# Hybrid decoder trunk, one core: group norm by tokens inside the chunk loop, decode step and w_out interleaved, w_out's weights gone over twice

## The chip, the core and the metric

The kernel runs on one core of a Trainium2 chip. The metric is device time in microseconds for one execution of the whole program: two decoder layers and a final norm.

The core has five engines with a queue each, in order: TensorE (PE, matmuls; PEld is its weight load), VectorE (DVE), ScalarE (ACT), GpSimd (POOL) and SyncE (SP, here the issuer of DMAs). They meet only through semaphores. Everything is float32; where a matmul carries weights, each operand is split into a high part (fp32r) and a low part, and three matmuls make one product: high x high, high weight x low activation, low weight x high activation.

## What is computed

Each layer, for 1024 prompt tokens and 8 sample tokens (a decode step) that share the weights:

```
h = rmsnorm(x); proj = h @ w_in
ya = rwkv7_mix(proj[:, :A_PROJ])          # recurrent state per head, 8 heads of 64
yb = sliding_window_attention(proj[:, A_PROJ:])
x = x + concat(ya, yb) @ w_out
h2 = rmsnorm(x); x = x + (silu(h2 @ w_gate) * (h2 @ w_up)) @ w_down
```

The end of `rwkv7_mix` is what moves. `y` is what the state scan reads out per token and head:

```
mean = mean(y over the 64 of a head); var = mean((y - mean)^2)
yn = (y - mean) * rsqrt(var + LNX_EPS) * lnx_g + lnx_b
bonus = sum(r * k * r_k over the head) * v
out = (yn + bonus) * g
```

The sample tokens have a state each (8 x 8 heads x 64 x 64), which takes one step of the same recurrence.

## The kernel before

Activations lie with channels on the 128 partitions and the T = 1032 tokens (1024 prompt, 8 sample) along the free axis. T is cut in three columns of CW = 344 tokens; `cs(c)` is a column. A weight unit is 128 x 1024. SP loads it (`fill_dma`), ScalarE casts its high part (`fill_high`), POOL subtracts the low part (`fill_low`), in a ring of three slots, so unit k + 3 takes the slot of unit k. A `tile` is one unit against one column: 8 k-steps of three matmuls (lines 1455 to 1457), 24 in all.

A layer runs through these stages: w_in (21 units), rope and attention, the preparation of the scan (LoRAs, decays, an inversion of triangular blocks by elimination on VectorE), then the chunk loop (line 1770): 16 chunks of 64 tokens. In chunk n TensorE applies the state to the keys (s1), makes the grams of chunk n + 1, solves (s2), transposes keys and values for the next chunk (`keys`, `values`), forms the state's update (s3) and reads y out (lines 1806 and 1808, channels on the partitions). VectorE masks the grams (line 1215), adds and scales the state (lines 1249 and 1251: S_add, S_new). Until chunk 5 VectorE also runs the elimination for chunks 8 to 15.

After the loop three things follow one another. The decode step: SP loads the states (line 424), VectorE and TensorE go through them in two halves (`i` in 0, 1), with sums over a head's channels as matmuls against `bdones` (lines 1826, 1828, 1831). Then the group norm for all columns, in twelve pieces of 128 channels x 344 tokens: TensorE centres (line 1841), sums squares (1849) and spreads root and bonus back over the channels (1835); ScalarE squares and takes roots; VectorE multiplies and gates (1313 to 1317, 1298); ScalarE casts the high part (814), POOL subtracts the low part (518). Then w_out: 8 units, three columns each (line 1882). It waits for the last low part `fin_low11`; ScalarE's first w_out cast waits for it too (line 819).

Behind w_out VectorE adds each tile to the residual `x`, which SP has loaded back from memory (`x_back`, line 440), ScalarE squares it, VectorE sums the squares (`sum2`), and after the last unit the second norm follows column by column: `inverse` (a reciprocal), `normed`, a cast on ScalarE (`high2`), `low2`. FFN's first tile follows it k-step by k-step (line 1462).

FFN: 11 iterations of 6 units (gate and up for two halves j, then two units of w_down). Per half VectorE makes `mid` for three columns, then `mid_low` for three (lines 1403 to 1406). The down projection waits for `ff{i}_low1{c}` and puts its 24 results in two PSUM banks in turn (four in the last iteration), which VectorE's additions free (line 1415).

## Time and profile before

| | us |
|---|---|
| median of three runs | 3411.71 (3409.21 to 3415.93) |
| the profiled execution | 3412.88 |
| its span, first to last instruction | 3410.9 |
| TensorE busy | 3031.5 (89%) |
| VectorE busy | 1395.1 (41%) |
| ScalarE busy | 849.3 (25%) |
| POOL busy | 568.7 (17%) |
| mean granted TensorE clock | 0.917 |

Times within an execution count from the span's start. A timeline row has its start, its length, engine, line and operation, what it writes and reads, a count where rows are merged, and in brackets the engine's idle time before it and what ended that. TensorE's records are pipelined: the distance of two starts is the cost of a matmul, not a record's length. A float32 matmul leaves two records, a transposition or an fp32r matmul one.

### The profile page before, as it was taken

The page shows a single profiled execution, that of the slowest core. Times are in us where ns is not written, and L with a number is a line of the kernel's source. Part 1 is how long each engine was busy: PE and PEld are TensorE (multiplying, and loading weights), DVE is VectorE, ACT ScalarE, POOL GpSimd, SP SyncE. Part 2 cuts the span into 40 slices and gives each one's busy share as a digit, 9 for nine tenths or more (in the row PEclk, how much of TensorE's full clock was granted, in tenths as well). Part 3 has the DMA queues.
Part 4 walks back from the last instruction along what each step waited for, and adds up shares of the span by engine and source line. Part 5 has one row for each costly group of instructions (what it writes and reads, how often), then busy time and mean ns, then how long its engine had stood idle before and what let it go on. Part 6 is the DMA issues. An engine that isn't in the chain of part 4 may idle for free.

```text
span 3410.9 us, 49606 instructions
## 1 busy us (share of the span) xinstructions
PE 3031.5 (89%) x20894; PEld 2748.5 (81%) x20894; DVE 1395.1 (41%) x2435; ACT 849.3 (25%) x1799; POOL 568.7 (17%) x277
## 2 busy tenths in 40 slices
PE   7996766978999999999999977579789999999997
PEld 6994734853999999999999956358359999999997
DVE  5325549643342232222353275684434223222324
ACT  3102642422231111111321044424223211111112
POOL 2220000002122112121122100100021221221123
PEclk9998967985999999999999988679769999999998
DMA  3101010012111111111121100000121111111111
GB/s 118 46 25 50 0 37 7 2 46 93 44 45 50 44 44 46 48 45 49 65 70 47 42 21 7 31 7 2 70 81 38 50 50 38 50 50 44 44 47 53
DMA packets 49443, 149.13 MB, mean 44 GB/s; under 512 B 8912, under 2 KB 19152, under 8 KB 48208
## 3 DMA queue, kind: packets, MB, share of 16 engines
q1 hardware_dynamic: 49232, 146.07, 13.0%
q8 instruction: 163, 2.67, 0.3%
q14 instruction: 48, 0.39, 0.0%
HBM read 128.52 MB, written 17.54 MB: 43 GB/s over the span
## 4 chain that ended last, share of the span: by engine, by line
PE 81%; DVE 12%; ACT 3%; issue 2%; DMA 1%; SPq 0%; POOL 0%; ACTq 0%; DVEq 0%
PE bank L1455 21%; PE bank L1457 20%; PE bank L1456 20%; PE bank L1835 2%; PE bank L1530 2%; PE bank L1562 1%; PE bank L1680 1%; PE bank L1808 1%; PE bank L1806 1%; PE bank L1523 1%; PE bank L1788 1%; PE bank L1841 1%; PE bank L1711 1%; PE bank L1798 1%; PE bank L1622 1%
## 5 line engine op out<-in xcount | busy, mean ns | idle before, releaser
L1455 PE MATMUL bank<-act_high,w_high 128*128 128x344 f32 x3504 | 1129.9, 322 | 36.0 <-POOL w_low L472 31.6
L1457 PE MATMUL bank<-act_high,w_low 128*128 128x344 f32 x3504 | 1122.1, 320 | 0.0
L1456 PE MATMUL bank<-act_low,w_high 128*128 128x344 f32 x3504 | 1121.6, 320 | 0.0
L472 POOL TENSOR_TENSOR w_low<-w_raw,w_high 128x1024 fp32r<-128x1024 f32 x190 | 483.5, 2552 | 1678.1 <-ACT w_high L547 1678.1
L1455 PEld LDWEIGHTS bank<-act_high,w_high 128*128 128x128 f32 x3504 | 662.3, 189 | 44.7 <-issue 19.2
L1456 PEld LDWEIGHTS bank<-act_low,w_high 128*128 128x128 f32 x3504 | 661.0, 189 | 1.3 <-issue 0.9
L1457 PEld LDWEIGHTS bank<-act_high,w_low 128*128 128x128 f32 x3504 | 661.7, 189 | 0.0
L1357 DVE TENSOR_TENSOR f_mid<-f_silu,bank 128x344 f32<-128x344 f32 x132 | 67.6, 512 | 849.5 <-PE bank L1457 849.5
L1455 PE MATMUL bank<-f_mid_high,w_high 128*128 128x344 f32 x1056 | 340.8, 323 | 27.2 <-DVE f_mid_low L1362 24.7
L1415 DVE TENSOR_TENSOR resid<-bank,resid 128x344 f32<-128x344 f32 x528 | 272.4, 516 | 223.7 <-PE bank L1457 223.7
L1457 PE MATMUL bank<-f_mid_high,w_low 128*128 128x344 f32 x1056 | 339.5, 321 | 0.0
L1456 PE MATMUL bank<-f_mid_low,w_high 128*128 128x344 f32 x1056 | 336.6, 319 | 0.0
L547 ACT CAST w_high<-w_raw 128x1024 fp32r<-128x1024 f32 x190 | 195.8, 1043 | 511.7 <-PE bank L1457 506.8
L1455 PEld LDWEIGHTS bank<-f_mid_high,w_high 128*128 128x128 f32 x1056 | 198.2, 188 | 33.6 <-issue 32.8
L1456 PEld LDWEIGHTS bank<-f_mid_low,w_high 128*128 128x128 f32 x1056 | 198.3, 188 | 0.2
L1457 PEld LDWEIGHTS bank<-f_mid_high,w_low 128*128 128x128 f32 x1056 | 198.2, 188 | 0.0
L976 DVE TENSOR_TENSOR proj<-bank,s_rstd 128x344 f32<-128x344 f32 x126 | 64.2, 515 | 290.7 <-PE bank L1457 290.7
L856 ACT CAST f_mid_high<-f_mid 128x344 fp32r<-128x344 f32 x132 | 63.3, 480 | 407.6 <-DVE f_mid L1357 407.6
L849 ACT ACTIVATE f_silu<-bank 128x344 f32<-128x344 f32 x132 | 60.0, 457 | 339.1 <-PE bank L1457 339.0
L1530 PE MATMUL bank<-a_k_twice,a_q_spread 128*128 (+1 forms) x256 | 73.1, 438 | 15.8 <-ACT a_q_spread L622 15.1
L1328 DVE TENSOR_TENSOR resid<-bank,resid 128x344 f32<-128x344 f32 x48 | 24.6, 513 | 144.8 <-PE bank L1457 144.8
L1215 DVE TENSOR_TENSOR c_gram<-bank,consts 128x512 f32<-128x512 f32 x64 | 41.2, 685 | 97.1 <-PE bank L1680 97.0
(273 smaller groups left out, 3104.5 us busy)
## 6 DMA issues: line engine op xcount, KB each, us to landing
w_raw<-wts SPq DMA_DIRECT2D x190, 512.0 KB, 3.5
resid<-x SPq DMA_DIRECT2D x3, 1376.0 KB, 11.1
att_keep<-act_low SPq DMA_DIRECT2D x2, 2064.0 KB, 10.6
att_low_back<-att_keep SPq DMA_DIRECT2D x2, 2064.0 KB, 9.4
resid<-x SPq DMA_DIRECT2D x8, 516.0 KB, 6.4
x_keep<-resid SPq DMA_DIRECT2D x3, 1376.0 KB, 5.7
resid<-x_keep SPq DMA_DIRECT2D x8, 516.0 KB, 6.7
o_y<-resid SPq DMA_DIRECT2D x3, 1376.0 KB, 5.7
```

Of the source, the lines that this page charges most:

```text
L472: eng.tensor_tensor(wl[s][:, :], raw[s][:, :], wh[s][:, :].bitcast(F32), ALU.subtract).then_inc(w_low, 1)
L547: eng.copy(wh[s][:, :], raw[s][:, :]).then_inc(w_high, 1)
L849: a(sil[:, c, :], bank[c][:, 0:CW], ACT.Silu).then_inc(scalar_steps, e.step(f"ff{i}_sil{j}{c}"))
L856: eng.copy(mh[:, j, cs(c)], midf[:, c, :]).then_inc(scalar_steps, e.step(f"ff{i}_high{j}{c}"))
L976: tt(proj[:, k, cs(c)], bank[3 * (k % 2) + c][:, 0:CW], rstd[:, c, :], ALU.mult).then_inc(vector_steps, e.step(f"win_ev{k}{c}"))
L1357: tt(midf[:, c, :], sil[:, c, :], bank[3 + c][:, 0:CW], ALU.mult).then_inc(vector_steps, e.step(f"ff{i}_mid{j}{c}"))
L1415: tt(x[:, k, cs(c)], bank[(DOWN_LAST if i == NR - 1 else DOWN)[n % (4 if i == NR - 1 else 2)]][:, 0:CW], x[:, k, cs(c)], ALU.add).then_inc ...
L1455: mm(out, wh[s][:, wcols], act_h, start=start, stop=False)
L1456: mm(out, wh[s][:, wcols], act_l, start=False, stop=False)
L1457: return mm(out, wl[s][:, wcols], act_h, start=False, stop=stop)
L1530: last = mm(bank[p][:, 256 * h:256 * h + 256], bdq[:, p, 128 * h:128 * h + 128], kd[:, p // 2, bass.ds((n + 1) * WIN, 2 * WIN)], start=Tru ...
L1835: return mm(bank[b][:, 0:CW], c_("spread")[0:8, 128 * o:128 * o + 128], rows, start=True, stop=True)
```

## The change

*Readout and group norm.* In the chunk loop y is read out with the 64 tokens on the partitions (operands swapped; the two heads of a pair in two runs with a wait, `yr`, between them). Two chunks make a block m of 128 tokens x 512 channels. VectorE centres it (`y_centre`), ScalarE squares it (`y_square`), VectorE sums (`y_variance`), ScalarE takes the root (`y_root`), VectorE scales, multiplies with a gain that SP has loaded in 128 rows (`lgr`) and adds bonus times v (`y_norm`); TensorE transposes back (`tokens_back`, bank 2), VectorE adds the bias and gates (`y_gate`). VectorE's pieces stand between the grams and S_add, gate and `bonus_v` behind S_new. Blocks 0 to 5 go in chunks 6 to 14, blocks 6 and 7 behind the loop. Column 0's and 1's high parts are cast and low parts subtracted there as well. The attention's low half comes back from memory by three DMAs from POOL's queue straight to its place, instead of one of SP's and a copy. The bonus sums ahead of the loop become 32 matmuls with the tokens as weights (`ctok`).

*Decode step.* Its states are loaded during the loop, and its pieces stand between the tiles of w_out on TensorE, and between additions and square sums on VectorE. Its own group norm for 8 tokens is 32 columns wide, with three small products (`dn_`).

*w_out.* Columns 0 and 1 for all eight units, then all eight units again for column 2. The second norm of columns 0 and 1 lies beside the second pass. The list of weight units has w_out twice, 103 units a layer instead of 95.

*FFN.* `mid` of columns 0 and 1, low half of column 0, `mid` of column 2, then the other two low halves.

```diff
@@ TensorE, behind the loop
-                eng.wait_ge(pool_steps, e.at("fin_low11"))
-                eng.wait_ge(scalar_steps, e.at("fin_high11"))
-                eng.wait_ge(pool_steps, e.at("att_low_back"))
-                for k in range(KT):
-                    s = unit(l, NIN + k)
-                    for c in range(NC3):
...
+                tokens_back(6)
+                eng.wait_ge(vector_steps, e.at(f"S_new{NCH - 1}"))
+                eng.wait_ge(scalar_steps, e.at(f"y_ev{NCH - 1}"))
+                dec_sums(0, 0)
+                out_column(0, 0)
+                dec_sums(0, 1)
+                eng.wait_ge(vector_steps, e.at("y_gated6"))
+                tokens_back(7)
+                out_column(0, 1)
+                out_column(1, 0)
+                dec_read(0)
+                out_column(1, 1)
+                dec_sums(1, 0)
+                dec_sums(1, 1)
+                out_column(2, 0)
+                out_column(2, 1)
+                dec_read(1)
+                out_column(3, 0)
+                eng.wait_ge(vector_steps, e.at("y_gated7"))
+                eng.wait_ge(vector_steps, e.at("dec_y11"))
+                mm(bank[2][:, 0:32], c_("centre"), dy[:, :], start=True, stop=True).then_inc(tensor_steps, e.step("dn_centred"))
...
+                out_column(3, 1)
+                eng.wait_ge(vector_steps, e.at("dn_squares"))
+                eng.wait_ge(vector_steps, e.at("dn_bonus_v"))
+                mm(bank[2][:, 64:96], bdones, dsq[:, :], start=True, stop=True).then_inc(tensor_steps, e.step("dn_var"))
+                for k in range(4, KT):
+                    out_column(k, 0)
+                    out_column(k, 1)
+                out_column(0, 2)
+                for c in range(2):
+                    eng.wait_ge(vector_steps, e.at(f"n2_sum{KT - 1}{c}"))
+                    square_sum("n2", c, 6 + c)
+                for k in range(1, KT):
+                    out_column(k, 2)
@@ TensorE, readout in the loop
-                    for o in range(4):
-                        for h in range(2):
-                            mm(bank[5 - h][HEAD[h], 64 * o:64 * o + 64], St[q][HEAD[h], o, :], r_dn(o)[HEAD[h], tk(n)], start=True, stop=False)
-                        for h in range(2):
-                            last = mm(bank[5 - h][HEAD[h], 64 * o:64 * o + 64], AV[q][:, h, o, :], GM[q][:, h, o, 64:128], start=False, stop=True)
+                    for h in range(2):
+                        if h:
+                            eng.wait_ge(tensor_steps, e.at(f"yr{n}_0"))
+                        for o in range(4):
+                            last = mm(bank[5 - q][HEAD[q], 128 * o + 64 * h:128 * o + 64 * h + 64], r_dn(o)[HEAD[h], tk(n)], St[q][HEAD[h], o, :],
+                                      start=(h == 0 and o == 0), stop=False, skip_group_check=True)
+                        last.then_inc(tensor_steps, e.step(f"yr{n}_{h}"))
+                        for o in range(4):
+                            last = mm(bank[5 - q][HEAD[q], 128 * o + 64 * h:128 * o + 64 * h + 64], GM[q][:, h, o, 64:128], AV[q][:, h, o, :],
+                                      start=False, stop=(h == 1 and o == 3), skip_group_check=True)
...
+                    if n in NORM_AT:
+                        eng.wait_ge(scalar_steps, e.at(f"bk_ev{n + 1}"))
+                        tokens_back(NORM_AT[n])
@@ VectorE, in the loop ahead of S_add, and behind S_new
+                    if n in NORM_AT:
+                        y_norm(NORM_AT[n])
+                    if n in SQUARE_AT:
+                        y_variance(SQUARE_AT[n])
+                    if n in CENTRE_AT:
+                        y_centre(CENTRE_AT[n])
...
+                    if n % 2 and n + 1 < NCH:
+                        bonus_v((n + 1) // 2)
+                    if n in NORM_AT:
+                        y_gate(NORM_AT[n])
@@ where: chunk -> block
+        CENTRE_AT = {6: 0, 7: 1, 8: 2, 9: 3, 11: 4, 12: 5, 14: 6}
+        SQUARE_AT = {7: 0, 8: 1, 9: 2, 10: 3, 12: 4, 13: 5, 15: 6}
+        NORM_AT = {8: 0, 9: 1, 10: 2, 11: 3, 13: 4, 14: 5}
+        NORMED = (0, 3, 5, 7, 9, 12, 14, 16)
@@ VectorE, behind the loop
+                y_norm(6)
+                y_centre(7)
+                y_gate(6)
+                eng.wait_ge(state_in, e.at("state_in"))
+                eng.wait_ge(scalar_steps, e.at("wdec"))
+                dec_in(0, 0)
+                y_variance(7)
+                dec_in(0, 1)
+                y_norm(7)
+                dec_back(0, 0)
+                y_gate(7)
...
+                add_out(3, 0)
+                sum2(2, 1)
+                dec_bonus()
+                dec_y(1)
+                add_out(3, 1)
+                sum2(3, 0)
+                dec_squares()
+                add_out(4, 0)
+                sum2(3, 1)
+                dec_out()
...
+                eng.wait_ge(sample_out, e.at("sample_out"))
+                add_out(0, 2)
+                sum2(KT - 1, 1)
+                inverse("n2", 0)
+                normed(0, 0)
+                for k in range(1, KT):
+                    add_out(k, 2)
+                    if k > 1:
+                        sum2(k - 1, 2)
+                    for i in range(NORMED[k - 1], NORMED[k]):
+                        j = i + 1
+                        if j == KT:
+                            inverse("n2", 1)
+                        if j < 2 * KT:
+                            normed(j // KT, j % KT)
+                        low2(i // KT, i % KT)
@@ ScalarE, second pass of w_out
+                for k in range(KT):
+                    square(k, 2)
+                    fill_high(l, NIN + KT + 3 + k, used=f"wo_mm{k}2")
+                    if k == 0:
+                        root("n2", 0)
+                        root("n2", 1)
+                    else:
+                        for i in range(NORMED[k - 1], NORMED[k]):
+                            high2(i // KT, i % KT)
@@ POOL, from the loop on
+                for c in range(NC3):
+                    eng.wait_ge(tensor_steps, e.at(f"bkt{11 + 2 * c}"))
+                    eng.dma_start(hl[:, 4:8, cs(c)], kept_low[:, :, cs(c)]).then_inc(att_back[c], e.load(f"att_back{c}", f"att_back{c}"))
+                    if c < 2:
+                        for o in range(4):
+                            out_low(c, o)
...
+                fill_low(l, NIN)
+                eng.wait_ge(tensor_steps, e.at("yt7"))
+                fill_low(l, NIN + 1)
+                fill_low(l, NIN + 2)
@@ VectorE, FFN
-                            for c in range(NC3):
-                                mid(i, j, c)
-                            for c in range(NC3):
-                                mid_low(i, j, c)
+                            mid(i, j, 0)
+                            mid(i, j, 1)
+                            mid_low(i, j, 0)
+                            mid(i, j, 2)
+                            mid_low(i, j, 1)
+                            mid_low(i, j, 2)
```

## Rows read from the trace of the kernel before

**Rows 1.** The page: the engines' shares of the chain that ended last.

```profile
PE 81%; DVE 12%; ACT 3%; issue 2%; DMA 1%; SPq 0%; POOL 0%; ACTq 0%; DVEq 0%
```

**Rows 2.** Table by stretches: length; busy (records) PE, PEld, DVE, ACT, POOL; clock; DMA.

```profile
726.00:840.00 114.00, 80.91 (x120) 28.00 (x120) 56.86 (x91) 22.52 (x45) 16.92 (x15) 0.57 0.15 58
840.00:933.00 93.00, 92.89 (x578) 92.66 (x578) 22.36 (x43) 18.19 (x31) 21.42 (x9) 0.98 0.27 94
```

**Rows 3.** TensorE's timeline, layer 0: last readout, w_out's start, FFN's second tile.

```profile
725.46 0.34 PE L1808 MATMUL bank<-c_gram,c_SA_V 128*64 128x64 f32 x4
...
840.11 0.63 PE L1455 MATMUL bank<-act_high,w_high 128*128 128x344 f32 x1 [6.86 <-POOL w_low L472]
...
844.11 0.32 PE L1457 MATMUL bank<-act_high,w_low 128*128 128x344 f32 x1
844.27 0.32 PE L1455 MATMUL bank<-act_high,w_high 128*128 128x344 f32 x1
...
942.53 0.32 PE L1455 MATMUL bank<-act_high,w_high 128*128 128x344 f32 x1
```

**Rows 4.** TensorE's timeline, layer 1: w_out's start.

```profile
2522.92 0.63 PE L1455 MATMUL bank<-act_high,w_high 128*128 128x344 f32 x1 [6.86 <-POOL w_low L472]
```

**Rows 5.** Timeline, decode step: a product over 512 columns, a reduction of 512.

```profile
732.33 2.08 PE L1826 MATMUL bank<-d_t_a,consts 128*128 128x512 f32 x2 [6.53 <-DVE d_t_a L1267]
...
747.51 0.68 DVE L1290 TENSOR_REDUCE y_heads<-d_t_a 128x8 f32<-128x512 f32 x1
```

**Rows 6.** Timeline ahead of the loop, and in chunks 14 and 15.

```profile
573.17 0.63 PE L1727 MATMUL bank<-c_Tt,c_NX 32*32 32x32 f32 x8 [7.55 <-DVE c_Tt L1183]
...
714.15 1.29 DVE L1215 TENSOR_TENSOR c_gram<-bank,consts 128x512 f32<-128x512 f32 x2 [5.07 <-PE bank L1680]
714.92 0.66 PE L1689 MATMUL bank<-consts,bk_heads 128*128 128x128 f32 x4
716.51 0.42 DVE L1249 TENSOR_TENSOR c_S<-bank,c_S 128x256 f32<-128x256 f32 x1 [1.08 <-PE bank L1798]
720.35 0.68 PE L1777 MATMUL bank<-c_S,ar_heads 64*64 64x64 f32 x16
```

**Rows 7.** Timeline: table load, cast, low parts on POOL, unit, norm of a column.

```profile
774.89 1.28 ACT L804 ACT_TABLE_LOAD   x1
...
835.55 0.91 POOL L518 TENSOR_TENSOR act_low<-d_fin_out,act_high 128x344 fp32r<-128x344 f32 x1 [1.52 <-ACT act_high L814]
...
922.30 1.03 ACT L547 CAST w_high<-w_raw 128x1024 fp32r<-128x1024 f32 x1
923.41 2.39 POOL L472 TENSOR_TENSOR w_low<-w_raw,w_high 128x1024 fp32r<-128x1024 f32 x1 [8.91 <-ACT w_high L547]
930.06 2.30 DVE L922 RECIPROCAL s_rstd<-n_std 128x344 f32<-128x344 f32 x1 [3.04 <-ACT n_std L559]
934.84 0.52 DVE L1347 TENSOR_TENSOR act_low<-n_normed,act_high 128x344 fp32r<-128x344 f32 x1
...
935.76 0.51 DVE L1347 TENSOR_TENSOR act_low<-n_normed,act_high 128x344 fp32r<-128x344 f32 x1
```

**Rows 8.** TensorE's timeline, chunks 13 and 14: readout, state update.

```profile
708.45 0.33 PE L1806 MATMUL bank<-ar_heads,c_S 64*64 64x64 f32 x4
...
708.97 0.33 PE L1806 MATMUL bank<-ar_heads,c_S 64*64 64x64 f32 x4
...
715.51 0.97 PE L1798 MATMUL bank<-c_SA_V,c_BK_t 128*64 128x64 f32 x16
```

**Rows 9.** TensorE's timeline, chunk 6, behind a wait.

```profile
642.50 1.12 PE L1777 MATMUL bank<-c_S,ar_heads 64*64 64x64 f32 x16 [2.07 <-DVE c_S L1251]
643.54 2.08 PE L1680 MATMUL bank<-ar_heads,bk_heads 64*128 64x128 f32 x16
```

**Rows 10.** TensorE's waits of the whole span; VectorE's timeline in FFN.

```profile
PE bank L1455 <- DVE f_mid_low L1362: 24.7, 20, 1.2
...
1124.26 1.36 DVE L1362 TENSOR_TENSOR f_mid_low<-f_mid,f_mid_high 128x344 fp32r<-128x344 f32 x3
```

498 lines of the change are left out of this document (271 added, 227 removed).

## The prediction, made before the changed kernel was run

> **What bounds the kernel now.** I began with the chain that ended last: TensorE holds 81% of it, VectorE 12% [rows 1], so a microsecond counts only where TensorE waits or works slowly. The table by stretches shows such a place: between the last chunk's readout and w_out, 114 us in which TensorE has 81 us of busy records at a mean granted clock of 0.57, and VectorE 57 us; then w_out, 93 us, full at 0.98 [rows 2]. TensorE's timeline gives the borders: the last readout of layer 0 is issued at 725.5 and done at 725.8, w_out starts at 840.1, and the second FFN tile starts at 942.5, so that the first is through [rows 3]. I call 725.8 the zero: w_out starts at 114.3 and the first FFN tile is through at 216.7. Layer 1 shows the same 6.86 us wait for the same POOL operation in front of its w_out [rows 4], and the borders lie equally far apart. Within the 102.4 us from 840.1 to 942.5 there are 25 tiles of 24 matmuls, each 0.16 us after the last (844.11 to 844.27) [rows 3]; with 0.157, to which the 93 us and 578 records of w_out come without their slow start [rows 2], that is 94.2 us; the other 8.2 are 1.9 of half clock at the start, about 0.6 of column sums and 5.7 in which FFN's first tile follows its norm on VectorE.
>
> **The change, part by part.**
>
> *1. Group norm in the chunk loop.* The loop is bound by TensorE from chunk 6 on, so two things count: what TensorE gets, and whether VectorE's new work comes late. Per pair of chunks VectorE gets a sum, a centring, a sum of squares, three products or sums of 512 columns, a reciprocal of 8 columns, four gate operations of 128 columns and one product with v. A 512-column operation takes 0.68 [rows 5]; in a chain of waits I count 0.72. Ahead of S_add, in the fullest chunks (8 and 9), stand a norm (0.15 + 3 x 0.72), a variance (0.65) and a centring (1.4): 4.3 us. What room is there: the grams end at 715.44, the state's two steps take 0.42 each and a little, and the next state matmuls start at 720.35 [rows 6]. That leaves 4.9 - 0.9 = 4.0 us, plus 0.6 as TensorE itself gets later. So these chunks come out even or lose some tenths; the others have at most 3.6 us. Gates and the product with v lie behind S_new, where VectorE sits idle 5.07 us before the next grams [rows 6], and take 1.9. In the chunks up to 5 VectorE is the bound; two products with v (1.4 us) go there, into small gaps: +0.3. TensorE gets a transposition back in six chunks, 4 records like the 0.6 us of keys [rows 6]: +3.5. ScalarE gets a table load for the root inside the loop, 1.28 us [rows 7], of which I count 1.0; squares and roots (about 0.8) nearly fit its gaps.
>
> The readout itself swaps operands: tokens on the output's partitions, 32 records as before, but in four runs instead of eight alternations. No row shows this form. The alternation now costs 0.52 for 8 records, 0.065 each (708.45 to 708.97); runs of 64x64 that alternate the row halves take 0.68 for 16, those that don't alternate 0.97 for 16, 0.056 at the pitch [rows 6, 8]. So the readout costs 1.8 us instead of 2.1 by the non-alternating row, and 2.4 if the loss of the alternation is added to the present cost: -0.3 to +0.3 per chunk, -3 to +3 for chunks 6 to 15. I take 0, since the rows pull both ways. The Trainium skill, TensorEngine Tiling (Array Packing), Key Properties, says that changing the tiling mode drains the array; four runs change it half as often, and by that alone the sum would be 3 us a layer lower. The same page's Gotcha 1 says that row tiles cannot use one PSUM bank at the same time, which the new form would make them do, and which its extra wait (yr) avoids; by that the lower end is not to be had. Sum of the loop: 0.3 + 3.5 + 1.0 + about 0.4 = 5 us a layer, from 0 to 14 (0.7 us more in each of ten chunks, if ScalarE's or VectorE's additions come late), **10 in all**.
>
> Ahead of the loop the bonus becomes 32 small matmuls with a full weight load each. At half clock that may cost 10 us more; TensorE waits 7.55 us for VectorE's transposes there [rows 6] and again before the first chunk's s0, which VectorE sets as well, so I cost it at nothing; without that cover it would be 10. r_dec is one small copy on VectorE's chain, 0.2.
>
> *2. From the last readout to w_out.* New order, from zero: ScalarE copies y and takes the root, 0.9; VectorE norms pair 6, 3.3, and centres pair 7, 4.75; ScalarE squares, then casts the four high parts of column 1, 5.3 to 6.95, then the first unit (1.03 [rows 7]) to 7.9. POOL, whose queue holds the four low parts ahead of the units, does 4 x 0.91 [rows 7] from 5.8 to 9.4, issues the third piece of the attention's low half, and needs 2.39 for the first w_low [rows 7]: w_out starts at about **13** instead of 114.3. POOL issues no DMA in the trace; its cost lies between 0 and that of POOL's nearest operation, 2.4; I take 1.0. The Trainium skill, DMA: Bandwidth & Descriptors, Specifications, gives about 1 us to the first byte on that path; no run here shows it. SP's queue passes the unit loads behind y15 alone, no longer behind the decode state's store; they land 3.5 us later, before ScalarE asks.
>
> *3. Decode step beside w_out.* Its 12 products of 512 columns stay on TensorE: two records took 2.08 at half clock [rows 5], so 0.86 each at full, 10.3 us. Transposition of pair 7 and three small products: 1.5; two column sums 0.6. TensorE's queue is in order, so waits in it hold up w_out. I walked both queues:
> - The sums of pair 1 wait for VectorE's inputs, 0.3; the second readout (dec_read) waits 0.9.
> - Before dn_centred TensorE waits for dec_y11. At that moment VectorE still has an addition, a square sum, two small operations, two products and two reductions (0.45 + 0.45 + 0.35 + 4 x 0.66): 4.1 us.
> - Before dn_var it waits for an addition, a sum and five small ones: 1.8.
> - After a wait of 2.07 us the same kernel got the half clock, 16 matmuls at 1.12 instead of 0.68 and the next at 2.08 [rows 6, 9]; for the 4.1 us wait I count 1.7.
> - The column sum of c = 1 waits for an addition queued before it: 0.7.
>
> *4. w_out's third column in a second pass.* TensorE work is the same; eight more units are loaded, cast (1.03) and subtracted (2.39) against 3.77 us of matmuls each, so POOL keeps up. But VectorE now does the norm of columns 0 and 1 here: per unit an addition, a sum and two or three pairs at 0.92 (934.84 to 935.76) [rows 7], and the first low half waits for ScalarE, which must first square and cast a unit: 4.15 to 5.0 us per unit against 3.77, and one reciprocal of 2.30 [rows 7] in between. VectorE ends some 7 us behind; units are three ahead, so TensorE sees it only at FFN's first two or three units: 3.5 us. In return the 5.7 us of FFN's slow first tile go.
>
> *Sum for a layer:* 13.0 + 94.2 + 1.9 + 10.3 + 1.5 + 0.6 + (0.3 + 0.9 + 4.1 + 1.8 + 0.7 + 3.5) + 1.7 = 134.5 against 216.7: 82 saved, **164 in two layers**. Without any of these waits it would be 95; with twice as many, 69.
>
> *5. FFN: low half of column 0 ahead.* TensorE waits 1.2 us for the low half in front of a down projection, 20 times, 24.7 us in all [rows 10], of the 22 down projections. In the new order that half is done while u of column 2 still runs, so 1.4 us of delay go. What is late next: VectorE does the other two low halves (three took 1.36 together [rows 10]) before its first addition, which frees the first of two banks; that comes 0.45 late. Net 0.95 x 22 = **21**, from 15 to 28.
>
> The profiled execution took 3412.9 us, 2.0 more than its span and 1.2 over the median shown. 3412.9 - 164 - 21 + 10 = 3238; as a median, **3237**.
>
> **Rivals.**
> (a) *The loop becomes VectorE's*: the ten chunks 6 to 15 each wait 2 us for S_new and lose 1.2 us to the clock: + 2 x 32 = 3301. For it: room of 4.0 against work of 4.3. Against: only two chunks are that full. 0.07.
> (b) *The decode step isn't beside w_out but between its tiles*: it takes its present 39 us (VectorE's chain) with w_out merely cutting it up. Then 39 instead of the 19 counted: 3237 + 40 = 3277. 0.08.
> (c) *The FFN edit does nothing* because the first addition takes the wait's place in full: 3258. 0.08.
> (d) *Slower*: the waits in w_out's queue hold TensorE at 1.2 GHz through the whole stage. 107 us of matmuls then take 107 more per layer: 3237 + 214 = 3451. It decides from 88 us per layer on, half of the 175 gained. Speaking for it: 0.57 in the stretch that has waits now; against: in w_out the granted clock is 0.98 after one slow start [rows 2], and between the waits stand whole tiles. 0.02.
>
> **How the numbers follow.** My forecast holds 0.75: 3237. Its own range: loop -10 to +18, w_out -26 to +27, FFN -7 to +6, not all at one end: 3205 to 3270. With (b) and (c) inside, **3205 to 3280**. 0.2% (7 us) is about what a measurement of this kernel can tell from no change; faster 0.97, same 0.01, slower 0.02.
>
> **What would show it.** w_out's first matmul some 13 us after the last readout; about 134 us from there to the second FFN tile; a 4 us wait of the `centre` product for the decode's reduction; the chunks from 6 on at 8.5 to 9.1 us; TensorE's waits for the low half of f_mid gone and a smaller one for an addition instead. I would be wrong if the chunks run over 9.5 us, if the stretch after the readout has TensorE at half clock, or if w_out waits for POOL.

## The result, and the profile after

The changed kernel takes 3289.23 us (median of four, 3287.30 to 3291.35) against 3411.15 (four, 3409.21 to 3415.93): ratio 0.9641, 95% interval 0.9624 to 0.9657, 122 us faster. The forecast was 3237, from 3205 to 3280: the sign is right, the gain was put 52 us too high, and the time lies outside the range. The profiled execution took 3289.88 us, 2.0 more than its span.

Busy time by engine, and the chain of waits by engine, of the changed kernel (they answer [rows 1]):

```profile
PE 2954.0 (90%) x20858; PEld 2779.5 (85%) x20858; DVE 1464.9 (45%) x2549; ACT 840.2 (26%) x1759; POOL 609.1 (19%) x297
...
PE 76%; DVE 13%; issue 5%; ACT 4%; DMA 1%; POOL 0%; SPq 0%; DVEq 0%; ACTq 0%; POOLq 0%
```

TensorE has 78 us less work on record than before, but its share of the chain fell from 81% to 76%: more of what is left is waiting. The table by stretches for layer 0 (it answers [rows 2]): last chunk; last readout to w_out; w_out's columns 0 and 1 with the decode step; second pass; the FFN's first tiles.

```profile
core 0: us, PE busy (x) PEld busy (x) DVE busy (x) ACT busy (x) POOL busy (x), PEclk, DMA share, GB/s
736.62:742.42 5.80, 5.15 (x80) 4.49 (x80) 1.54 (x3) 1.85 (x6) 0.00 (x0) 1.00 0.00 1
742.42:757.84 15.42, 4.44 (x8) 1.59 (x8) 14.14 (x20) 6.14 (x11) 9.52 (x6) 0.74 0.79 285
757.84:842.93 85.09, 78.16 (x415) 71.85 (x416) 40.46 (x78) 15.65 (x27) 25.86 (x13) 0.91 0.31 100
842.93:883.06 40.13, 32.55 (x199) 30.69 (x197) 29.34 (x36) 15.26 (x27) 16.59 (x7) 1.00 0.26 81
883.06:911.43 28.37, 23.22 (x122) 22.21 (x123) 22.11 (x37) 14.75 (x25) 4.71 (x2) 0.88 0.19 57
```

The empty 114 us are gone: 15.4 are left. TensorE now idles somewhat in each of the later stretches, and most in the second pass, 7.6 of 40.1 us. Its timeline, only rows with one of the longer waits (they answer the borders of [rows 3]; the first row is the last readout):

```profile
741.70 0.68 PE L1974 MATMUL bank<-c_SA_V,c_gram 128*64 128x64 f32 x8
745.86 0.69 PE L1916 MATMUL bank<-consts,y_normed 128*128 128x128 f32 x4 [3.48 <-DVE y_normed L1298]
748.91 2.04 PE L1995 MATMUL bank<-d_t_a,consts 128*128 128x512 f32 x2 [2.36 <-ACT act_high L808]
...
757.84 0.66 PE L1606 MATMUL bank<-act_high,w_high 128*128 128x344 f32 x1 [5.18 <-POOL w_low L491]
...
802.09 0.61 PE L2037 MATMUL bank<-d_y,consts 128*128 128x32 f32 x2 [3.91 <-DVE d_y L1404]
...
810.87 0.38 PE L2043 MATMUL bank<-d_squares,consts 128*128 128x32 f32 x2 [1.72 <-DVE d_bonus L1420]
...
864.34 0.43 PE L1606 MATMUL bank<-act_high,w_high 128*128 128x344 f32 x1 [0.35 <-POOL w_low L491]
...
870.42 0.43 PE L1606 MATMUL bank<-act_high,w_high 128*128 128x344 f32 x1 [2.05 <-POOL w_low L491]
...
876.50 0.43 PE L1606 MATMUL bank<-act_high,w_high 128*128 128x344 f32 x1 [2.04 <-POOL w_low L491]
...
883.06 0.62 PE L1606 MATMUL bank<-act_high,w_high 128*128 128x344 f32 x1 [2.52 <-issue]
...
891.73 0.42 PE L1606 MATMUL bank<-act_high,w_high 128*128 128x344 f32 x1 [3.19 <-DVE resid L1440]
```

The zero is 742.4 here. w_out starts 15.4 us later (forecast 13.0), the second FFN tile 149.3 us later (forecast 134.5, before 216.7); in layer 1 it is 14.3 and 146.3. This account follows from the same borders in both layers. The loop runs from the first state product of the chunk loop to that of the last chunk; the FFN's rest is what lies behind the start of its seventh tile, up to the next layer's loop or to the end:

| part, us against before | forecast | layer 0 | layer 1 |
|---|---|---|---|
| ahead of the first loop | 0 | -2.0 | |
| loop and last readout | +5 each | +18.6 | +12.0 |
| last readout to second FFN tile | -82 each | -67.4 | -70.4 |
| second to seventh FFN tile | 0 | +4.1 | +4.1 |
| rest of the FFN | -10.5 each | -10.7 | -11.3 |

The column sums of both layers give -123.0, the difference of the two spans (3410.9 and 3287.9). So 21 of the missing 52 us lie in the loop and its last readout, 34 between the last readout and the FFN's seventh tile; the FFN's rest and the stretch ahead of the loop give 3 back.

The list of TensorE's waits (us in total, times, longest); the row of L1566 answers the 24.7 us of [rows 10], 20 times, now 4.0:

```profile
PE bank L1606 <- POOL w_low L491: 35.6, 9, 17.5
...
PE bank L2037 <- DVE d_y L1404: 7.8, 2, 3.9
...
PE bank L1606 <- DVE resid L1440: 6.3, 2, 3.2
...
PE bank L1950 <- ACT c_SA L822: 4.5, 6, 1.2
...
PE bank L1606 <- DVE resid L1566: 4.0, 20, 0.2
PE bank L1606 <- ACT f_silu L893: 3.9, 2, 1.9
...
PE bank L2043 <- DVE d_bonus L1420: 3.4, 2, 1.7
```

Two readings of the trace gave the theories that were tried.

*VectorE and POOL.* VectorE's and POOL's timelines in the second pass:

```profile
861.89 2.39 POOL L491 TENSOR_TENSOR w_low<-w_raw,w_high 128x1024 fp32r<-128x1024 f32 x1 [4.65 <-ACT w_high L580]
...
860.22 0.57 DVE L1454 SCALAR_TENSOR_TENSOR n_normed<-resid,params,s_rstd 128x344 f32<-128x344 f32 x1
862.23 2.43 DVE L1459 TENSOR_TENSOR act_low<-n_normed,act_high 128x344 fp32r<-128x344 f32 x1 [1.44 <-ACT act_high L884]
...
865.07 0.50 DVE L1459 TENSOR_TENSOR act_low<-n_normed,act_high 128x344 fp32r<-128x344 f32 x1
```

The same subtraction takes 0.50 us, and 2.43 where POOL's subtraction of w_low started 0.34 us earlier; it ends 0.4 us behind POOL's. Twelve of these operations in two layers show it, and two of n_normed with 2.07. A unit with two normalised tiles takes VectorE 6.1 us in the second pass: 2.76 of its own work, 1.45 of waiting for ScalarE's cast, 1.9 for POOL; the others take 6.5 to 7.0. Ahead of w_out POOL is held as well: its four low parts take 6.44 us beside the decode products (5.25 in layer 1), and 3.87 at 824.95, where VectorE has little to do.

```profile
748.25 6.44 POOL L534 TENSOR_TENSOR act_low<-proj,act_high 128x344 fp32r<-128x344 f32 x4 [17.21 <-ACT act_high L808]
754.63 0.78 POOL L540 DMA_DIRECT2D act_low<-att_keep  x1
755.44 2.35 POOL L491 TENSOR_TENSOR w_low<-w_raw,w_high 128x1024 fp32r<-128x1024 f32 x1
...
824.95 3.87 POOL L534 TENSOR_TENSOR act_low<-proj,act_high 128x344 fp32r<-128x344 f32 x4
```

*The clock in the loop.* A stretch of half clock (1.2 GHz) lies in each layer's loop: 23.9 us from 640.5 in layer 0, beside a wait of 1.40 us for S_new ahead of chunk 6, and 13.7 us from 2289.2 in layer 1, 2 us behind the 1.17 us wait for ScalarE's table load in chunk 8. Layer 1 waits 1.36 us ahead of its chunk 6 too, and there no half clock follows. A chunk that begins at half clock takes 14.4 to 14.8 us; the same chunks take 8.6 and 9.3 without it (below). Before, a wait of 2.07 us at the same place was followed by 3.4 us of half clock. The stretches ahead of, in and behind that of layer 0:

```profile
621.00:640.50 19.50, 19.32 (x339) 17.20 (x335) 18.12 (x25) 8.93 (x26) 0.00 (x0) 1.00 0.01 3
640.50:664.40 23.90, 22.68 (x220) 20.20 (x220) 8.29 (x15) 6.75 (x18) 0.00 (x0) 0.50 0.13 46
664.40:683.00 18.60, 17.43 (x289) 15.42 (x288) 10.30 (x22) 10.17 (x26) 0.00 (x0) 1.00 0.01 2
```

### The profile page after: what moved, and what is told of

Read it like the earlier page. It is cut to its first block, busy times and chain, and to the rows that moved or that the text cites. A ratio compares the mean times of both kernels' runs of the same rounds, so it can differ in the third digit from the quotient of the medians.

```text
span 3287.9 us, 49756 instructions
## 1 busy us (share of the span) xinstructions
PE 2954.0 (90%) x20858; PEld 2779.5 (85%) x20858; DVE 1464.9 (45%) x2549; ACT 840.2 (26%) x1759; POOL 609.1 (19%) x297
## 4 chain that ended last, share of the span: by engine, by line
PE 76%; DVE 13%; issue 5%; ACT 4%; DMA 1%; POOL 0%; SPq 0%; DVEq 0%; ACTq 0%; POOLq 0%
PE bank L1606 20%; PE bank L1608 20%; PE bank L1607 20%; PE bank L1681 2%; PE bank L1713 2%; PE bank L1674 1%; PE bank L1974 1%; PE bank L1970 1%; PE bank L1831 1%; PE bank L1950 1%; PE bank L1773 1%; PE bank L1865 1%; PE bank L1960 1%; DVE c_T L1226 1%; DVE c_NT L1224 1%
## 5 line engine op out<-in xcount | busy, mean ns | idle before, releaser
L491 POOL TENSOR_TENSOR w_low<-w_raw,w_high 128x1024 fp32r<-128x1024 f32 x206 | 521.9, 2539 | 1678.5 <-ACT w_high L580 1661.5
L1566 DVE TENSOR_TENSOR resid<-bank,resid 128x344 f32<-128x344 f32 x528 | 270.4, 516 | 209.8 <-PE bank L1608 209.8
L580 ACT CAST w_high<-w_raw 128x1024 fp32r<-128x1024 f32 x206 | 212.5, 1043 | 490.2 <-PE bank L1608 487.1
L1606 PEld LDWEIGHTS bank<-f_mid_high,w_high 128*128 128x128 f32 x1056 | 198.1, 188 | 10.7 <-DVE resid L1566 10.1
L1681 PE MATMUL bank<-a_k_twice,a_q_spread 128*128 (+1 forms) x256 | 71.7, 432 | 15.4 <-ACT a_q_spread L655 14.8
L1681 PEld LDWEIGHTS bank<-a_k_twice,a_q_spread 128*128 128x128 f32 x256 | 53.0, 217 | 27.1 <-ACT a_q_spread L655 15.5
## 6 DMA issues: line engine op xcount, KB each, us to landing
att_keep<-act_low SPq DMA_DIRECT2D x2, 2064.0 KB, 10.7
```

Source lines behind the costliest of these rows:

```text
L491: eng.tensor_tensor(wl[s][:, :], raw[s][:, :], wh[s][:, :].bitcast(F32), ALU.subtract).then_inc(w_low, 1)
L580: eng.copy(wh[s][:, :], raw[s][:, :]).then_inc(w_high, 1)
L1566: tt(x[:, k, cs(c)], bank[(DOWN_LAST if i == NR - 1 else DOWN)[n % (4 if i == NR - 1 else 2)]][:, 0:CW], x[:, k, cs(c)], ALU.add).then_inc ...
L1606: mm(out, wh[s][:, wcols], act_h, start=start, stop=False)
L1681: last = mm(bank[p][:, 256 * h:256 * h + 256], bdq[:, p, 128 * h:128 * h + 128], kd[:, p // 2, bass.ds((n + 1) * WIN, 2 * WIN)], start=Tru ...
```

## The experiments

Times and ratios of the following kernels stand against the kernel before, run on the same chip in the same rounds. 3289 is the changed kernel, which wasn't run again in these rounds; the medians of the kernel before lie between 3411.15 and 3414.49 in them, so a difference to 3289 of a few us says little unless the trace shows where it lies.

### The FFN's order alone (ffn_alone)

```diff
-                            for c in range(NC3):
-                                mid(i, j, c)
-                            for c in range(NC3):
-                                mid_low(i, j, c)
+                            mid(i, j, 0)
+                            mid(i, j, 1)
+                            mid_low(i, j, 0)
+                            mid(i, j, 2)
+                            mid_low(i, j, 1)
+                            mid_low(i, j, 2)
```

> The kernel before with the new order of the FFN's products and low halves on VectorE, and nothing else of the change. In the changed kernel TensorE's 24.7 us of waits for f_mid_low in front of the down projections are gone, and 4.0 us of waits for the first addition stand in their place (20 times 0.2 us). Theory (step 5 of the prediction, with that smaller second wait): 20.7 to 23 us less, 3388 to 3390 us. Rival (c), the edit does nothing because TensorE works slower after it by as much: within 7 us of 3411.

Measured: 3391.37 us (nine runs, 3385.17 to 3428.66), ratio 0.9945 (0.9913 to 0.9978). In its trace the layers are 11.3 and 11.4 us shorter from the last readout to the next layer's loop, or to the end, 22.7 in all, and TensorE's waits for f_mid_low are replaced by 20 waits of 0.2 us for the first addition. Step 5 stands, rival (c) falls. The profiled execution itself took 3404.16 us: layer 0's loop, which lies ahead of everything that the edit touches, has 51 us at a granted clock of 0.53. The rows of the wait and of that stretch:

```profile
PE bank L1457 <- DVE resid L1417: 4.0, 20, 0.2
...
600.40:651.70 51.30, 51.30 (x556) 44.02 (x555) 34.59 (x64) 16.80 (x48) 0.00 (x0) 0.53 0.01 2
```

TensorE is busy throughout that stretch and just ahead of it: here half clock came without any wait that the trace shows.

### The readout's order alone (readout_runs)

```diff
-                    for o in range(4):
-                        for h in range(2):
-                            mm(bank[5 - h]..., St[q]..., r_dn(o)..., start=True, stop=False)
-                        for h in range(2):
-                            last = mm(bank[5 - h]..., AV[q]..., GM[q]..., start=False, stop=True)
+                    for h in range(2):
+                        for o in range(4):
+                            mm(bank[5 - h]..., St[q]..., r_dn(o)..., start=(o == 0), stop=False)
+                        for o in range(4):
+                            last = mm(bank[5 - h]..., AV[q]..., GM[q]..., start=False, stop=(o == 3))
```

> The kernel before with only the order of its readout changed: per half of the heads four products with the state, then four with the gram, four runs of one shape instead of eight changes of shape; operands and banks stay as they were. In the changed kernel the readout takes 2.43 us a chunk against 2.10 before, in four runs of 0.61. Theory 1: the order makes that cost (each run of eight records 0.61 instead of 0.52): about 0.33 us more a chunk, 32 chunks, of which the 20 chunks from 6 on and the reaction of the others count: 7 to 11 us more, 3418 to 3422 us. Theory 2: not the order but the swapped operands (tokens on the output's partitions, all eight into one bank) cost it: the readout stays at 2.1 us or gets shorter, and the time stays within 7 us of 3411. On the clock: if the long half-clock stretch of the changed kernel (23.9 us after a wait of 1.40 us in layer 0) comes from the readout's runs, it shows here too after the 2.07 us wait in chunk 6, with 10 to 15 us more a layer; if not, the stretch stays at 3.4 us.

Measured: 3419.03 us, ratio 1.0024 (1.0004 to 1.0043). Undisturbed chunks take 8.64 and 9.08 us, as in the changed kernel, instead of 8.32 and 8.76. Two of the four runs of a readout in its trace:

```profile
715.69 0.68 PE L1806 MATMUL bank<-ar_heads,c_S 64*64 64x64 f32 x8
716.30 0.68 PE L1809 MATMUL bank<-c_gram,c_SA_V 128*64 128x64 f32 x8
```

Eight records every 0.605 us, against 0.52 in [rows 8]: theory 1. The operands' swap costs nothing of its own. The clock is not decided by it: half clock for 20.5 us beside a wait of 1.40 us in layer 0's loop, none beside 1.33 at the same place in layer 1's.

### The root's table ahead of the loop (table_ahead)

```diff
+                a(yss[:, 0:1], eps_lnx, ACT.Sqrt).then_inc(scalar_steps, e.step())
                 eng.wait_ge(tensor_steps, e.at("ctok"))
```

> The changed kernel with one root of one column on ScalarE put ahead of the chunk loop, so that the root's table is loaded there and not in chunk 8. Theory: the two waits of 1.17 us for ScalarE's copy behind the table load go, and with the one of layer 1 (2287.1) the 13.65 us of half clock that begin beside it, worth 5 to 7 us: 7 to 10 us less, 3279 to 3282 us. Rival: the half clock comes at this place whatever the wait is (in layer 0 it follows a 1.40 us wait two chunks earlier): only the two waits go, 2.3 us less, 3287 us, and the half clock of layer 1 starts elsewhere in the loop.

Measured: 3285.07 us (3277.53 to 3292.84), ratio 0.9615 (0.9588 to 0.9641), some 4 us less. The wait in chunk 8 is gone (9.28 us instead of 10.57), but half clock now begins at chunk 6 in both layers' loops of the profiled execution, 20.5 us each. This wait alone is not what brings the half clock; the wait ahead of chunk 6 is still there. The median stands for neither theory nor rival: three of the six runs take 3277.5 to 3279.9 us at a mean granted clock of 0.931 to 0.934, the profiled one and two others 3290.3 to 3292.8 at 0.926 to 0.927. So half clock doesn't seem to follow that wait in every execution; only the profiled one shows where it lies.

### No waits in the loop (no_waits_in_loop)

The edit above, and:

```diff
-                    elif n == 5:
-                        for h in range(2):
-                            blocks_out(1, h, 0)
...
                         bonus_v((n + 1) // 2)
+                    if n == 5:
+                        for h in range(2):
+                            blocks_out(1, h, 0)
```

> The changed kernel with two edits in the chunk loop: the root's table loaded ahead of the loop, and two of VectorE's transpositions of chunk 5 (3.83 us together) behind the new state instead of in front of it. In the changed kernel TensorE waits 1.4 us ahead of chunk 6 and 1.17 in chunk 8, and the half clock lasts 23.9 us from chunk 6 on in layer 0 and 13.65 from chunk 8 on in layer 1; chunks take 14.4 to 14.8 us there instead of 8.6 to 9.1. Theory: the waits set the half clock off; without them chunks 5 to 9 run at 8.6 to 9.7 us in both layers and the loop (first to last state product) takes about 139 us instead of 151 and 147: 21 us less, 3268 us (3265 to 3272). Rival: the half clock comes in this loop by itself (TensorE's many small products), with or without these waits: 5 us less, 3284 us, and a stretch of half clock of 10 us or more remains in at least one layer's loop.

Measured: 3268.70 us (3267.23 to 3269.74), ratio 0.9563 (0.9524 to 0.9601), 20.5 us less, the theory's sum. Both loops take 138.9 us, 20.6 less together. That the total agrees is in part luck: in the profiled executions half clock in the last chunk takes 5.0 of it back (below), and the stretches from the last readout to the seventh FFN tile are 5.1 shorter, for which there was no forecast and is no explanation. The same three stretches of layer 0 as above:

```profile
621.00:640.50 19.50, 19.50 (x337) 17.37 (x334) 18.21 (x24) 9.04 (x26) 0.00 (x0) 1.00 0.06 10
640.50:664.40 23.90, 23.90 (x398) 21.21 (x396) 13.75 (x25) 10.87 (x30) 0.00 (x0) 1.00 0.10 40
664.40:683.00 18.60, 18.60 (x300) 16.36 (x296) 14.23 (x31) 9.49 (x26) 0.93 (x1) 1.00 0.13 32
```

The middle stretch holds 398 matmuls instead of 220, at full clock. Over all profiles of kernels that keep the chunk-6 wait and have the new readout, the changed kernel's and seven others', a stretch of 13.6 us or more begins at chunk 6 (ten times) or 8 (six times) in each of 16 loops; without the waits, here and in all_together, in none of four. So in this form of the loop the long stretch of half clock comes with these waits and goes with them; the wait ahead of chunk 6 alone didn't set it off in six of the 16. In the last chunk it still came: 8.3 us from its state product to the end of the readout in both layers of this run, instead of 5.8. There the longest wait is 0.46 us, and in ffn_alone there was none: a long wait is not the only way into half clock.

### POOL's subtraction cut down in the second pass (second_pass_no_low)

```diff
-                    fill_low(l, k)
+                    fill_low(l, k, 8 if NIN + KT + 3 <= k < NIN + 2 * KT + 3 else U)
```

> The changed kernel, in which POOL subtracts only 8 of the 1024 columns for the low half of the eight units that are cast during w_out's second pass (the low halves of these units are left out, so the FFN's first products are computed with wrong low halves; a POOL subtraction then takes a few tenths instead of 2.39 us). In the changed kernel twelve of VectorE's subtractions for act_low take 2.39 to 2.44 us, each beside a POOL subtraction of w_low; the others take 0.50. Theory 1: VectorE and POOL exclude each other there, VectorE's operation waits until POOL's ends: then all of VectorE's subtractions take 0.5 us, a unit of the second pass goes from 6.1 to about 4.2 us, and TensorE's waits for w_low of 0.35, 2.05, 2.04, 2.5 and 3.19 us a layer go, with some 1.5 us of half clock twice: 26 us less in two layers, 3263 us (from 3258 to 3270). Theory 2: ScalarE's order (square, unit, then the cast that VectorE waits for) sets the pace, and the long subtractions are no cause: unit 6.1 less 0.3 us, time at most 7 us less.

Measured: 3267.43 us (3264.09 to 3269.76), ratio 0.9563 (0.9534 to 0.9593), 22 less. All of VectorE's subtractions take 0.5 us, as this one, whose wait for the cast is as long as in the changed kernel:

```profile
861.42 0.52 DVE L1459 TENSOR_TENSOR act_low<-n_normed,act_high 128x344 fp32r<-128x344 f32 x1 [1.45 <-ACT act_high L884]
```

Units with two tiles follow each other at 4.2, the others at 4.6 to 5.1, and no wait for w_low is left in the second pass. Theory 1. At the FFN's first tiles 1.74 us of waiting for an addition and 2.8 for ScalarE's silu are left: these are not POOL's. It doesn't yet say whether POOL holds VectorE through the operands or otherwise; the next two do.

### The casts ahead of the weights on ScalarE (casts_first)

```diff
                     square(k, 2)
+                    for i in range(NORMED[k - 1] if k else 0, NORMED[k]):
+                        high2(i // KT, i % KT)
                     fill_high(l, NIN + KT + 3 + k, used=f"wo_mm{k}2")
...
-                    else:
-                        for i in range(NORMED[k - 1], NORMED[k]):
-                            high2(i // KT, i % KT)
```

> The changed kernel with another order on ScalarE in w_out's second pass: the casts of the norm's high parts, on which VectorE's subtractions wait, stand ahead of the cast of the next weights, not behind it. A unit takes VectorE 6.1 us there: 2.76 of its own operations, 1.45 of waiting for these casts, 1.9 in which its subtraction stands beside POOL's subtraction of w_low. Theory (VectorE and POOL exclude each other, and ScalarE's order makes the wait): the 1.45 fall to about 0.4, POOL's subtraction starts 0.9 us later and now meets another operation of VectorE (the sum of squares), so the exclusion stays; 5.2 to 5.3 us a unit, 6 to 7 us less a layer in TensorE's waits for w_low, with some half clock 13 to 18 us less: 3274 us (3271 to 3278). Rival: POOL's later start costs VectorE as much as the earlier casts give, 5.9 to 6.1 us a unit and at most 5 us less.

Measured: 3281.01 us (3275.81 to 3283.66), ratio 0.9593 (0.9553 to 0.9632): 8 less, between the two. VectorE's and POOL's rows:

```profile
860.12 0.51 DVE L1439 TENSOR_TENSOR resid<-bank,resid 128x344 f32<-128x344 f32 x1
860.54 2.35 DVE L1446 TENSOR_TENSOR n_square_sum<-n_square_sum,n_square 128x344 f32<-128x344 f32 x1
...
860.14 2.39 POOL L491 TENSOR_TENSOR w_low<-w_raw,w_high 128x1024 fp32r<-128x1024 f32 x1 [2.73 <-ACT w_high L580]
```

The wait for the casts fell to 0.50, and the hold moved to another operation, as expected; units with two tiles take 5.1 to 5.4 us. Units with three tiles or with the reciprocal take 6.2 and 6.9, which the forecast left out, so the mean of five is 5.8, against 6.4 in the changed kernel. The first row is new: the addition that reads one operand from a bank isn't held, the sum that reads both from SBUF is.

### Operands in PSUM (operands_in_psum)

```diff
+        hnp = lambda c, k: bank[(2, 5)[k % 2]][:, 0:CW] if c < 2 else hn[:, k, :]
+        rsp = lambda c: bank[6 + c][:, 0:CW] if c < 2 else rstd[:, c, :]
...
-                    tt(acc[:, c, :], acc[:, c, :], sqk[:, c, :], ALU.add)...
+                    tt(acc[:, c, :], acc[:, c, :], bank[4][:, 0:CW] if c == 2 else sqk[:, c, :], ALU.add)...
-                    stt(hn[:, k, :], x[:, k, cs(c)], pc("fn", k), rstd[:, c, :], ALU.mult, ALU.mult)...
+                    stt(hnp(c, k), x[:, k, cs(c)], pc("fn", k), rsp(c), ALU.mult, ALU.mult)...
-                    tt(hl[:, k, cs(c)], hn[:, k, :], hh[:, k, cs(c)].bitcast(F32), ALU.subtract)...
+                    tt(hl[:, k, cs(c)], hnp(c, k), hh[:, k, cs(c)].bitcast(F32), ALU.subtract)...
...
```

Left out: ScalarE's square writes that bank and its cast reads the tiles from theirs, the reciprocal writes its bank, and a normalised tile waits for the low half two tiles back, since two banks take turns.

> The changed kernel with the same operations in the same order, but in w_out's second pass three kinds of operand lie in PSUM banks that are free there instead of SBUF: the squares of column 2, the reciprocal roots of columns 0 and 1, and their normalised tiles. So each of VectorE's operations of that pass reads at most one tile from SBUF. Theory (VectorE is held by POOL only where it reads two tiles from SBUF; its addition of a bank to resid takes 0.52 us even beside a POOL subtraction, 846.99): no operation of VectorE takes 2.4 us there any more although POOL's subtractions stay at 2.39; a unit takes 4.2 us instead of 6.1, and the waits for w_low of a layer go: 3267 us (3263 to 3272), as in the run in which POOL's subtraction was left out. Rival: every operation of VectorE that touches SBUF can be held: units of about 6 us, within 5 us of 3289.

Measured: 3272.10 us (3269.96 to 3275.98), ratio 0.9592 (0.9577 to 0.9607): 17 less, 0.1 us above the expected range, with all of POOL's work in place. In the profiled executions the two stretches from the last readout to the seventh FFN tile are 21.8 us shorter than in the changed kernel (18.9 in second_pass_no_low); what is missing lies in other stretches. Units with two tiles take 4.4 us, and VectorE's additions and subtractions in the pass take 0.50 to 0.58 us:

```profile
862.17 2.41 POOL L493 TENSOR_TENSOR w_low<-w_raw,w_high 128x1024 fp32r<-128x1024 f32 x1 [1.95 <-ACT w_high L582]
...
862.47 0.52 DVE L1464 TENSOR_TENSOR act_low<-bank,act_high 128x344 fp32r<-128x344 f32 x1 [1.41 <-ACT act_high L886]
863.09 0.58 DVE L1459 SCALAR_TENSOR_TENSOR bank<-resid,params,bank 128x344 f32<-128x344 f32 x1
...
864.43 0.50 DVE L1449 TENSOR_TENSOR n_square_sum<-n_square_sum,bank 128x344 f32<-128x344 f32 x1
```

Beside a POOL subtraction of 2.41 us VectorE's operations run at their own 0.5. What VectorE reads decides: two tiles from SBUF and it is held, one and it isn't. That settles the second pass; of the waits for w_low 1.5 us a layer is left, at the FFN's second tile.

### The first unit ahead of column 1's parts (first_unit_ahead)

```diff
+                eng.wait_ge(vector_steps, e.at(f"S_new{NCH - 1}"))
+                fill_high(l, NIN)
                 y_square(7)
...
                     out_high(1, o)
-                fill_high(l, NIN)
                 y_root(7)
...
                 for c in range(NC3):
+                    if c == 1:
+                        eng.sem_inc(pool_idle, 1)
+                        fill_low(l, NIN)
...
                             out_low(c, o)
-                eng.sem_inc(pool_idle, 1)
-                fill_low(l, NIN)
```

> The changed kernel with w_out's first unit (its cast on ScalarE, its subtraction on POOL) ahead of the four high and low parts of column 1, which only the second tile needs. In the changed kernel w_out starts 15.4 us after the last readout: POOL's four low parts take 6.44 us there instead of the 3.87 they take alone (824.95), beside VectorE's decode products, and the first w_low follows them. Theory: w_out starts 9 to 10 us after the last readout, its second tile 5.5 to 6 us earlier than now (now 766.3): 11 to 12 us less in two layers, 3278 us (3276 to 3283). Rival: POOL's subtraction, now beside the norm of pair 6 and the first decode products, holds VectorE up by as much (the two exclude each other), so that the transposition of pair 7, which comes in front of the second tile, isn't earlier: the first tile starts earlier, the second doesn't, within 4 us of 3289.

Measured: 3283.36 us (3280.51 to 3285.78), ratio 0.9605 (0.9565 to 0.9645): 6 less, half of the theory. w_out starts 13.5 us after the last readout instead of the 9 to 10 expected, its second tile 3.0 us earlier than in the changed kernel in layer 0 and 1.2 in layer 1. POOL and VectorE there:

```profile
745.63 2.36 POOL L491 TENSOR_TENSOR w_low<-w_raw,w_high 128x1024 fp32r<-128x1024 f32 x1 [17.35 <-ACT w_high L581]
...
748.72 3.50 POOL L534 TENSOR_TENSOR act_low<-proj,act_high 128x344 fp32r<-128x344 f32 x4
...
748.46 4.33 DVE L1376 TENSOR_TENSOR d_t_a<-consts,proj 128x512 f32<-128x512 f32 x1
```

Now VectorE is the one that is held, 4.33 us for a product of 0.68, until all four of POOL's subtractions are through, and TensorE has the decode sums, which wait for that product, in front of the tile. The rival's mechanism is there, at half its price.

### The small norm products later (norm_products_later)

```diff
-                    eng.wait_ge(tensor_steps, e.at("dn_centred"))
+                    eng.wait_ge(tensor_steps, e.at("dn_bonus"))
...
+                out_column(3, 1)
                 eng.wait_ge(vector_steps, e.at("y_gated7"))
                 eng.wait_ge(vector_steps, e.at("dec_y11"))
                 mm(bank[2][:, 0:32], c_("centre"), dy[:, :], start=True, stop=True).then_inc(tensor_steps, e.step("dn_centred"))
...
-                out_column(3, 1)
+                out_column(4, 0)
                 eng.wait_ge(vector_steps, e.at("dn_squares"))
...
-                for k in range(4, KT):
+                out_column(4, 1)
+                for k in range(5, KT):
```

> The changed kernel with the decode step's three small products one tile later in TensorE's queue: centring and bonus behind the second tile of unit 3, the variance behind the first tile of unit 4. In the changed kernel TensorE waits 3.9 us in front of the centring and 1.7 in front of the variance, and the tiles behind these waits run 2.2 and 1.6 us longer at half clock. Theory: both waits and the half clock behind them go but for some 0.4 us: 9 us a layer, 18 in all, 3271 us (3269 to 3277). Rival: VectorE's chain is what counts, and the wait shows up again further back (the column sums, the first low halves): at most 8 us less.

Measured: 3267.90 us (3263.48 to 3274.29), ratio 0.9565 (0.9523 to 0.9606), 21 less: slightly more than the theory. The profiled executions are 25.7 us apart; 17.0 of it lie between the last readout and the FFN's seventh tile, which is the edit's and just under the theory's 18, and 4.3 in layer 0's loop (147.0 us instead of 151.3), which the edit doesn't touch, as it doesn't the rest. The waits of 3.9 and 1.7 us are 0.1 and 0, and the tiles behind run at full clock (3.7 us instead of 5.9 and 5.3). The centring, now without a wait:

```profile
794.63 0.38 PE L2038 MATMUL bank<-d_y,consts 128*128 128x32 f32 x2
```

Nothing came back further on.

### The start reordered, and all together (start_reordered, all_together)

TensorE's queue from the last readout on, in start_reordered:

```diff
+                out_column(0, 0)
+                tokens_back(7)
                 dec_sums(0, 0)
-                out_column(0, 0)
+                out_column(0, 1)
                 dec_sums(0, 1)
-                tokens_back(7)
-                out_column(0, 1)
                 out_column(1, 0)
+                out_column(1, 1)
                 dec_read(0)
-                out_column(1, 1)
```

Further on each piece of the decode step stands one tile later likewise; VectorE does `y_variance(7)` and `y_norm(7)` ahead of `dec_in(0, 0)`; ScalarE casts the first unit ahead of column 1's high parts; POOL issues both transfers, then takes the first unit, then column 1's low parts.

> The changed kernel with a new order from the last readout on: w_out's first unit and the norm of pair 7 ahead of the decode products on VectorE, POOL's transfers ahead of the unit, the first decode products one tile later in TensorE's queue, and the three small norm products later still, as in the run norm_products_later (21 us less). Theory: the norm of pair 7 and the first unit no longer meet the decode products; w_out's first tile starts 8 us after the last readout (now 15.4), the second after 14 (now 23.9): 9 to 10 us a layer, with the 21 together 40 us less: 3249 us (3243 to 3258). Rival: VectorE's decode chain, which begins later, comes late for the products that follow, and the gain of the start shows up as waits in front of them: 3262 us, the sum of the two runs before.

Measured: 3256.10 us (3251.28 to 3262.57), ratio 0.9547 (0.9533 to 0.9562). w_out starts 7.7 us after the last readout, and its second tile 15.4. What it waits for now is ScalarE, not POOL:

```profile
748.93 0.63 PE L1611 MATMUL bank<-act_high,w_high 128*128 128x344 f32 x1 [3.11 <-ACT act_high L810]
```

The gain is 33, halfway between the theory (40) and the rival (27). Up to the FFN's seventh tile the layers are 18.8 and 14.8 us shorter than in the changed kernel, and in norm_products_later 10.4 and 6.7; so the new start gives 16.5 of the 19 us that the theory counts for it, and 4 of the 40 were never this stretch's. The products behind it are not late: its trace has no wait of TensorE between w_out's first tile and the column sums above 0.2 us.

all_together joins start_reordered, casts_first, operands_in_psum and no_waits_in_loop.

> The changed kernel with all of it: no waits in the loop (20.5 us less), the casts first (with the operands in PSUM worth some 4 us instead of 8), the operands in PSUM (22), the new order of the start with the norm products later (40). Theory (the four places are independent): 86 us less, 3203 us (3196 to 3215). Rival: what the start gains is lost again where VectorE is late, in the column sums in front of the second pass and in the FFN's first tiles: 3220 us or more.

Measured: 3209.73 us (3205.56 to 3214.28), ratio 0.9405 (0.9392 to 0.9418), 79 us under the changed kernel and inside the theory's 3196 to 3215. The second FFN tile starts 119.2 and 119.8 us after the last readout. The edits alone gave 33, 8, 17 and 20.5: their sum, 79, is what they give together.

## Why the prediction was right and wrong

*Step 1, the loop: wrong by 21 us, 30.6 instead of 10.* Two terms failed. The readout was put at 0 with ends of -0.3 and +0.3 a chunk; it is +0.32, just above the upper end, in all 16 chunks and not only from 6 on: 10 us in two layers. The lower end came from a run of sixteen records that doesn't alternate, 0.056 us each [rows 8]. The prediction calls it a run of 64x64, but the row is one of 128x64, and its pitch doesn't hold for runs of eight, which take 0.076 each. By the Trainium skill, TensorEngine Tiling (Array Packing), Key Properties, each change of the tiling mode drains the array, so four runs should have been cheaper than eight alternations; the measurement is 2.42 us against 2.10. The second term, waits and clock, was counted at nothing beyond what stands in before: some 10 us in both loops (slowed chunks of 9.8 to 10.9 us instead of 8.3 and 8.8). It is 20.6, for loops of 151.3 and 147.2 us that take 138.9 without the waits: 5.1 of waits and 15.5 of half clock. So this term is 10.5 too small. The other terms of the loop came to the 10 us that were forecast: none of the fullest chunks waits for the state, TensorE's transposition costs 0.6 in four chunks, 0.8 in chunk 13, beside a wait of 0.63 for ScalarE, and 0.9 in chunk 14, the table load 1.2. The room of 4.0 us held; rival (a) fell. The sign of being wrong was named (chunks over 9.5 us), its cause was another.

*Step 2, the start of w_out: 15.4 and 14.3 instead of 13.0.* POOL's low parts start at 5.85 us, as worked out (5.8), and the transfer costs 0.78 (1.0). The term that failed is 4 x 0.91: it took 6.44 and 5.25, because VectorE's decode products and POOL's subtractions hold each other.

*Step 3, the decode step beside w_out: the waits are right, the clock isn't.* 3.9 and 1.7 (forecast 4.1 and 1.8), column sum 0.63 (0.7), dec_read 0.3 (0.9), pair 1 0.67 (0.3). The half clock behind the two long waits costs 2.2 and 1.6 us in layer 0, where 1.7 was counted for the first and nothing for the second. What wasn't asked is whether the waits need to be there: three small products one tile later, and 17 us go. Rival (b) fell: of the decode step's 39 us before, TensorE feels its 12 products and some 7 us of waits.

*Step 4, the second pass: wrong by some 12 us a layer.* The unit's 4.15 to 5.0 us were 6.1 to 7.0, and TensorE's waits at w_out's end and the FFN's first tiles 0.35 + 2.05 + 2.04 + 2.52 + 3.19 + 1.9 = 12 us instead of 3.5, with two more tiles at half clock (1.6 each) behind them. (The 2.52 is put down to issue; POOL's subtraction for that unit ends 0.1 us ahead of the tile.) The missing term is the hold between VectorE and POOL, 1.9 us in most units. Without it, in second_pass_no_low, the units take 4.2 to 5.1 us and the waits come to 4.5, near the forecast; the one for silu, 1.9 here, is not the hold's and stays. The hold could have been read in the trace of before, in a stretch that the argument didn't touch, at the end of layer 0, VectorE and POOL:

```profile
1703.67 0.57 DVE L927 SCALAR_TENSOR_TENSOR act_low<-resid,params,act_high 128x344 fp32r<-128x344 f32 x1
...
1704.62 7.79 DVE L927 SCALAR_TENSOR_TENSOR act_low<-resid,params,act_high 128x344 fp32r<-128x344 f32 x7
...
1706.33 5.21 POOL L472 TENSOR_TENSOR w_low<-w_raw,w_high 128x1024 fp32r<-128x1024 f32 x2 [21.93 <-ACT w_high L547]
```

Seven operations of 0.52 (3.7 us) took 7.79 where POOL has two subtractions. The Trainium skill, SBUF — State Buffer, SBUF: two separate sides, has the rule: a VectorE operation with two inputs in SBUF and a GpSimd operation that reads SBUF exclude each other, and the one that starts second waits for the whole instruction of the first. These runs agree: 2.43 against 0.50, and no hold with one operand in PSUM. One row doesn't follow the rule's order: in first_unit_ahead VectorE's product is recorded 0.26 us ahead of POOL's four subtractions and yet ends behind the last of them. This was the rule that spoke against this change, and the prediction cited others. The rows of the changed kernel show seven holds a layer, six of 1.9 us and one of 1.5: 13 us on VectorE.

*Step 5, the FFN: right.* 22.0 us instead of 21; the first addition comes 0.2 late, not 0.45. Rival (c) fell.

*Rival (d)* fell too: granted clock 0.91 in the pass with the waits, 1.00 in the second.

*The range.* It summed the ends of the costs that were listed. Of the 52 us, 21 lie in the loop: 10 of readout, 10.5 of waits and half clock. 34 lie behind it, up to the FFN's seventh tile: 19 to 22 went in the two runs without the hold in the second pass (18.9 and 21.8), 4 lie in the later start of w_out, some 3 in half clock behind the decode step's waits, and the remaining 5 to 8 weren't taken apart. 3 come back elsewhere. Neither the hold nor the half clock in the loop was on the list.
